# Five weight units rounded by a second, converting transfer instead of by ScalarE

## The reference, cut to what matters

```python
u = rmsnorm(h, norm_mix[l])
proj = u @ w_in[l]                                   # 1024 x 7168
q, k, v, g_ret, p, gates = jnp.split(proj, split_points, axis=-1)
q = rotary(q.reshape(b, s, RET_HEADS, RET_QK_DIM))
k = rotary(k.reshape(b, s, RET_HEADS, RET_QK_DIM)) * (RET_QK_DIM ** -0.5)
ret = retention(q, k, v)                             # chunks of 64, decay per head
ret = ret * lax.rsqrt(jnp.mean(ret * ret, axis=-1, keepdims=True) + NORM_EPS)
ret = ret.reshape(b, s, RET_V) * jax.nn.silu(g_ret)
pool_out = multiscale_pool(p, pool_w[l], pool_scale[l])
gate = jax.nn.sigmoid(gates.reshape(b, s, N_BRANCH, D_MODEL) + gate_bias[l])
merged = gate[:, :, 0] * (ret @ w_ret_up[l]) + gate[:, :, 1] * (pool_out @ w_pool_up[l])
h = h + merged @ w_out[l]
```

## Time and profile before

| | |
|---|---|
| time, median of 3 runs | 1195.98 us (1195.96 to 1196.49) |
| profiled execution: span from first to last instruction | 1194.3 us |
| TensorE matmuls | 99% of the span |
| VectorE | 77% |
| ScalarE | 57% |
| GpSimd | 14% |
| DMA | 220.76 MB, mean 185 GB/s |
| TensorE clock granted | 0.999 of full speed |

### The profile page before, as it was taken

How to read it: one execution, slowest core, us unless ns; L and a number is a source line. 1 busy time by engine, 2 the same in 40 slices (tenths; PEclk the granted TensorE clock), 3 DMA queues, 4 the chain that set the end, 5 groups by cost and what they waited for, 6 DMA issues and landing times.

```text
span 1194.3 us, 14398 instructions
## 1 busy us (share of the span) xinstructions
PE 1184.7 (99%) x5568; PEld 975.3 (82%) x5568; DVE 919.8 (77%) x1155; ACT 678.9 (57%) x822; POOL 165.2 (14%) x169
## 2 busy tenths in 40 slices
PE   9999999999999999999999999999999999999997
PEld 7777888888887888888888888888888888888886
DVE  7788898888778798877798878645577666988884
ACT  7775756656646666654666554545344545666552
POOL 2100132210200132210132120000000000222200
PEclk9999999999999999999999999999999999999999
DMA  8434565547333465556455555745544454555540
GB/s 340 177 138 156 182 237 198 183 177 271 128 120 131 187 229 184 185 181 235 148 198 189 182 207 212 276 162 187 204 154 153 159 176 171 189 206 181 188 177 36
DMA packets 32727, 220.76 MB, mean 185 GB/s; under 512 B 3761, under 2 KB 4273, under 8 KB 7058
## 3 DMA queue, kind: packets, MB, share of 16 engines
q1 hardware_dynamic: 32514, 219.64, 50.5%
q10 hardware_dynamic: 144, 0.20, 0.0%
HBM read 218.77 MB, written 1.05 MB: 184 GB/s over the span
## 4 chain that ended last, share of the span: by engine, by line
PE 98%; issue 0%; DVE 0%; DMA 0%; ACT 0%; SPq 0%; POOLq 0%; POOL 0%; DVEq 0%; ACTq 0%
PE ps L259 30%; PE ps L261 30%; PE ps L260 30%; PE ps L264 5%; PE ps L267 4%; DMA raw<-in_w 0%; DVE h L406 0%; DVE AR L2600 0%; DVE st L1812 0%; SPq L2622 0%; DVE AR L1830 0%; ACT whi L228 0%; ACT AR L2591 0%; POOLq L134 0%; POOL st L395 0%
## 5 line engine op out<-in xcount | busy, mean ns | idle before, releaser
L218 DVE SCALAR_TENSOR_TENSOR wlo<-raw,whi 128x2048 fp32r<-128x2048 f32 x160 | 366.4, 2295 | 116.4 <-ACT whi L211 89.0
L259 PE MATMUL ps<-whi,xh 128*128 128x512 f32 x1104 | 435.9, 395 | 0.0
L261 PE MATMUL ps<-whi,xl 128*128 128x512 f32 x1104 | 430.4, 390 | 0.0
L260 PE MATMUL ps<-wlo,xh 128*128 128x512 f32 x1104 | 430.1, 390 | 0.0
L211 ACT CAST whi<-raw 128x2048 fp32r<-128x2048 f32 x162 | 310.1, 1915 | 179.8 <-PE ps L261 178.1
L259 PEld LDWEIGHTS ps<-whi,xh 128*128 128x128 f32 x1104 | 207.2, 188 | 47.9 <-issue 1.4
L261 PEld LDWEIGHTS ps<-whi,xl 128*128 128x128 f32 x1104 | 207.2, 188 | 44.6
L260 PEld LDWEIGHTS ps<-wlo,xh 128*128 128x128 f32 x1104 | 207.5, 188 | 40.7
L259 PE MATMUL ps<-whi,yh 128*128 128x512 f32 x344 | 137.9, 401 | 0.0
L261 PE MATMUL ps<-whi,yl 128*128 128x512 f32 x344 | 134.4, 391 | 0.0
L260 PE MATMUL ps<-wlo,yh 128*128 128x512 f32 x344 | 133.9, 389 | 0.0
(11 more groups left out here) (249 smaller groups left out, 1213.1 us busy)
## 6 DMA issues: line engine op xcount, KB each, us to landing
raw<-in_w SPq DMA_DIRECT2D x198, 1024.0 KB, 4.8
raw<-in_w SPq DMA_DIRECT2D x4, 512.0 KB, 7.4
h<-in_x SPq DMA_DIRECT2D x4, 256.0 KB, 4.8
raw<-in_w SPq DMA_DIRECT2D x4, 256.0 KB, 4.3
AR<-in_b_pw SPq DMA_DIRECT2D x1, 1024.0 KB, 4.7
AR<-in_gate_bias SPq DMA_DIRECT2D x1, 1024.0 KB, 6.9
AR<-in_dft SPq DMA_DIRECT2D x1, 864.0 KB, 7.5
AR<-in_rmask SPq DMA_DIRECT2D x1, 768.0 KB, 8.5
```

Source lines behind the costliest of these rows:

```text
L218: e.scalar_tensor_tensor(out=wlo[:, v % S, :], in0=raw[:, v % R, :], scalar=1.0, in1=whi[:, v % S, :].bitcast(F32), op0=ALU.mult, op1=ALU. ...
L259: e.matmul(o, ah, bh, start=start, stop=False, skip_group_check=skip)
L260: e.matmul(o, ah, bl, start=False, stop=False, skip_group_check=skip)
L261: return e.matmul(o, al, bh, start=False, stop=stop, skip_group_check=skip)
```

## The change

For the second units of the chunks k0, q1, k1, gr0 and gr1 (units 20, 22, 24, 26 and 28) ScalarE's cast is left out. In its place GpSimd issues a DMA that reads the unit from memory once more and writes it into `whi`; as its source is float32 and its destination `fp32r`, the DMA converts. It waits for `used` of the unit four before, as the cast did, and signals on a semaphore of its slot (by 16). VectorE's `lo` of these units waits for that signal and, now itself, for the landing of `raw`. `raw` is still loaded by SyncE for them. GpSimd issues four of the DMAs between the input norm's power and those of the retention norm of heads 0 and 1, the fifth ahead of those of heads 2 and 3. The orders on the other engines are otherwise unchanged.

```diff
         def hi(e, q, v):
-            if v < NU:
+            if v < NU and v not in by_dma:
                 q.wait_ge(*sig.at("raw%d" % (v % R), v))
...
         def lo(e, q, v):
             if v < NU:
+                if v in by_dma:
+                    q.wait_ge(*sig.at("raw%d" % (v % R), v))
                 q.wait_ge(*sig.at("hi", v))
...
+        by_dma = [U["p"] + n for n in (20, 22, 24, 26, 28)]
+
+        def rounded(e, q, v):
+            q.wait_ge(*sig.at("used", v - S))
+            e.dma_start(whi[:, v % S, :], wst[v]).then_inc(*sig.up("rounded%d" % (v % S), v, by=16))
+            sig.alias("hi", (v,), "rounded%d" % (v % S), (v,))
...
         def gpsimd_ret(e, q):
             norm_pool(e, q, "nm", 1)
+            for key in ("v1", "q0", "k0", "q1"):
+                rounded(e, q, RU[key] + 5)
             gpsimd_ret_norm(e, q, 0)
+            rounded(e, q, RU["k1"] + 5)
             gpsimd_ret_norm(e, q, 1)
             norm_pool(e, q, "n2", 0)
```

## The result

The changed kernel takes 1203.49 us, median of 4 runs (1202.84 to 1203.61), against 1195.97 before (1195.83 to 1196.49, 4 runs): a ratio of 1.0059, 95% interval 1.0047 to 1.0071. It is slower, by 7.5 us where 5.0 were forecast. The profiled execution is the fastest of the four: a time of 1202.84 us with a span of 1201.1, 6.8 us over the span before. Its mean granted clock is 0.997; the three others have 0.996 and took 0.6 to 0.8 us more.

The account below looks back on a forecast made before the run. TensorE was taken as the bound, busy 90.00 of 90 us, so relieving ScalarE gains nothing. Waits of 1.2 + 1.0 + 2.8 = 5.0 us on 1195.98 gave 1201.0 us, range 1197.4 to 1208.5.

Parts of the forecast that it names:

- The time L from release to landing: Each added DMA, from release of its slot to landing: 4.7 + 1.0 + 1.3 = 7.0 us, ends 3.9 and 11.2.
- GpSimd's share: Term of L: GpSimd makes the DMA request by program, taken as 1.0 us on top of a load's 4.7.
- Company: Term of L: a raw load sharing the stream with the added DMA, taken as 1.3 us, half of 2.7.
- (a): Unit 20, second of k0: rotation of q0's first half ends 1.2 us late for TensorE; generally L - 5.8.
- (b): Unit 22: VectorE waits 1.1 us, but k0's rotation is ready with 0.9 us to spare; hidden from TensorE.
- (c): Unit 24: two masks behind the remainders of units 24 and 25 reach TensorE 1.0 us late.
- (d): Unit 26: remainder, retention norm, then k1's rotation, 2.8 us late for TensorE; L - 3.1 if (a) and (c) are gone.
- (e): Unit 28: DMA lands at 918.6, before VectorE comes to its remainder at 919.2; hidden, no wait.
- The quick transfer: Rival, chance 0.18: L at or under 5.6, only (d) left, 1.5 to 2.4 us, about 1198 us.
- The slow stream: Rival, 0.19 including held-up requests: converting halves the stream's rate, L 9.7, 10.4 us more, 1206.4 us.
- GpSimd's request held back by VectorE: Half of a rival, 0.04 of its 0.19: VectorE's running 2.29 us instruction delays the request; L 9.3, +9.6, 1205.6 us.
- the first DMA of GpSimd pay a start of its own: Rival within the forecast's range, no separate chance: extra start falls on (a); 2 us more at unit 20 makes the sum 7.0.

## Why the prediction was right, and where it was not

The direction, the bound on the gain and the place of the largest wait were right. ScalarE's 9.5 us brought nothing, the loss is TensorE's waiting and its consequence, and the longest wait is the one in front of k1's transposes. That the number came as near is in part luck: of three forecast waits one came, and it was as long as the three together. Of the signs that the prediction named, TensorE's 85.12 of 90 us and the place of the longest wait hold. Three new waits do not, nor do landings near 6 us and more (four of five took 4.9 to 5.5), and VectorE's waits for the DMAs were 4.1, 1.4, 1.1 and 5.4 us where 5, 1, 3 and 3 were put. By its steps:

- **The time L from release to landing.** Taken as 7.0 for all five. Measured from the chunk's end to VectorE's start it was 5.8 for unit 20 (857.65 to 863.45), 5.9 for unit 22, 5.4 for unit 24 and 8.2 for unit 26 (894.98 to 903.14). Of its terms, GpSimd's share was put at 1.0 us beyond the landing of a load and measured 0.4, with 0.3 to 0.4 from the chunk's end to the issue. Company was spread as 1.3 over all; it falls on the one that is issued second, 2.1 us for unit 26 by the experiment with unit 29 held, and hardly on the first. That is the mis-sized term. The order could be read beforehand, though not who pays for it: the load of unit 23 goes out 1.7 us behind the release of unit 20 (859.23 and 857.52; the prediction has 1.6), that of unit 29 behind the `lo` that ends at 893.76, ahead of the release of unit 26.
- **(a)** 1.2 us predicted, none measured. Its formula L - 5.8 gives 0.0 with L = 5.8, and gave the right wait when the DMA was made late (3.1 us).
- **(b)** Hidden, as predicted.
- **(c)** 1.0 us predicted, none measured. The formula L - 6.0 gives nothing with 5.4.
- **(d)** 2.8 us predicted, 4.9 measured. The formula for the case that (a) and (c) are gone was L - 3.1, and with 8.2 that is 5.1. The chain is the predicted one in each member. The kernel in which the remainder of unit 26 stands behind the norm shows that the wait needs this order: the landing took the same 7.8 us and nothing waited. The kernel with unit 29 held shows that its length follows the landing.
- **(e)** Hidden, as predicted.
- **The clock.** It is missing from the sum. The prediction priced a wait of TensorE at its own length ("by exactly what TensorE comes to wait"). It costs that and the matmuls at half speed behind it, 1.8 us here. Waits 5.0 (as forecast in sum, by two errors that cancel: 2.2 too much in (a) and (c), 2.1 too little in (d); the prediction's own list has 2.4 for L = 5.6 where L - 3.1 is 2.5) and 1.8 for the clock make 6.8 in the profiled execution.
- **The rivals.** The quick transfer (L under 5.6 everywhere) did not occur: unit 24 was the only one under it. But the picture that this rival drew, (d) as the only wait, is the one that came; it was unit 26's L of 8.2 that made it 4.9 us and not 1.5 to 2.4. The slow stream did not either; the converting transfer runs like a plain one. Nor was GpSimd's request held back by VectorE: the first two were issued (858.05 and 868.93) while a remainder of 2.29 us ran there (857.04 and 868.28), and their issues lasted 0.76 and 0.55 us and their landings 5.3 and 5.5. Nor did the first DMA of GpSimd pay a start of its own: its issue lasted 0.76 us against 0.54 and it landed after 5.3.

The time lies within the range, 2.5 us above the forecast. In the profiled execution the clock makes 1.8 of it; the other three have a lower mean clock (0.996) and no trace.

## What to carry to other kernels

Where TensorE has no waits, relieving another engine gains nothing, and the only question is which in-order queue the new, longer latency stands in: look for the work behind the waiting instruction that TensorE wants first, and move the wait behind it. Give each transfer its own latency by what is issued just ahead of it, not an average. And price a wait of TensorE of some 3 us or more above its own length: here 2.8 us cost 1.4 more, and 4.7 to 4.9 us cost 1.8 to 2.3 more, while one of 3.1 us cost nothing more in one execution.

## What the runs showed of the hardware

- Two transfers of 1 MB that overlap do not share evenly. The one issued ahead, by 0.2 to 1.7 us, loses 0.6 us at most (4.9 to 5.5 against 5.1 from GpSimd, 4.8 to 5.3 against 4.7 from SyncE). GpSimd's in second place took 7.0 to 8.1 us, 1.9 to 3.0 longer (the 8.1 with a third load beside it). SyncE's loads in second place in the changed kernel lose 1.4 to 2.1 (6.1 to 6.8 against 4.7). The stream in the 11 us from 893 to 904 of the changed kernel, in slices of 0.28 us, the load of unit 29 and the DMA of unit 26:

```profile
GB/s 0 0 0 0 0 0 30 328 119 60 328 387 357 447 447 447 328 417 298 328 298 209 387 357 447 447 387 417 209 89 30 30 30 30 0 0 0 0 0 0
```

The stream stands at 200 to 450 GB/s for some 5 us, and then a trickle of 30 GB/s lasts about a microsecond before the DMA counts as landed. So part of the second one's 7.8 us is a thin end and not the shared stream. Unit 26 has a shorter one even with unit 29 held, unit 28 has none; what makes it no trace here shows. The Trainium skill, "DMA: Bandwidth & Descriptors", section "Queues, rings and completion order", has each engine take the queues in turn, packet by packet; if two streams of 2.7 us took even turns, the first would lose what is left of its own when the second comes in: an estimated 1.4 us with a lead of 1.3 us, and 2.5 with a lead of 0.2. Here it lost 0.6 at most with the one lead, and 0.1 with the other (4.8 us for SyncE's load beside the late DMA of unit 20), so the traces do not bear even sharing out in these cases.

- Waits of TensorE of 2.8 us and more were followed by the half clock in the traces of three kernels (waits of 2.8, 4.7 and 4.9 us) and not in that of a fourth: after 3.1 us the profiled execution kept the full clock, while the other four of that kernel have a lower mean clock (0.997 to 0.998) and took 1.3 to 1.8 us more. With TensorE kept busy through the same time it stayed up in all five (mean clock 0.999 to 1.000).

- A DMA that converts float32 to the rounded format took as long as a plain one from the same engine, 5.1 us for 1 MB.
